# Transposing cached keys on VectorE in 32x32 blocks and scoring them as 32x32 products, in the decode attention of a hybrid decoder step

## The chip, the cores and the metric

One core of one Trainium2 chip runs the whole program; all data are f32. The metric is the device time of one execution in microseconds (us), the median of the runs. The core has TensorE (matrix products, out of weights that are loaded first; its results land in PSUM, 8 banks of 512 columns), VectorE, ScalarE and GpSimd for everything else, and DMA queues that SyncE (SP) and GpSimd fill.

## The reference, cut to what matters

The program is one layer of a decoder: RMS norm, one input projection, eight attention heads with forget gates beside eight RWKV-7 heads, an output projection, a SwiGLU network and a last norm. It is done for one prompt of 16 + 512 tokens and for eight running sequences of 8 new tokens each. The change is in the attention of the running sequences over their cached past:

```python
PAST_LEN = 4096; PAGE_SIZE = 128; FOX_HEADS = 8; HEAD_DIM = 64; DEC_BATCH = 8; DEC_SEQ = 8
k_past = cache_k[l][page_table].reshape(DB, n_pages * PAGE_SIZE, FOX_HEADS, HEAD_DIM)
v_past = cache_v[l][page_table].reshape(DB, n_pages * PAGE_SIZE, FOX_HEADS, HEAD_DIM)
s = jnp.einsum('bqhd,bkhd->bhqk', qf, k.astype(jnp.float32))
s = s + cq - jnp.swapaxes(c_k, 1, 2)[..., None, :]
p = jax.nn.softmax(jnp.concatenate(logits, axis=-1), axis=-1)
o = jnp.einsum('bhqk,bkhd->bqhd', p[..., start:start + n], v.astype(jnp.float32))
```

So for each of 8 sequences, 32 pages of 128 tokens (each 128 x 512 values of keys and as many of values) are read by number, and every page is scored against 8 heads x 8 queries.

## The kernel before

The program is written engine by engine, with semaphores, in these stages: the input projection and the prompt's attention (up to about 331 us), then the **lots stage** (335 to 912 us), then the output projection, the SwiGLU network (L1369, L1388, L1394) and the last norm.

**Lots.** The running sequences are taken in 4 pairs (`NPAIR`), each pair's 32 pages in 8 lots of 4 pages (`LOT`, `NLOT`), so 32 lots (`LOTS`). A page of a pair is a 128x512 tile for each of the two sequences (q). The 128 rows of scores are 2 sequences x 8 heads x 8 queries. In a lot TensorE does this:

- `turn_keys` (L1173) transposes each page with 4 products 128x128 by the identity into PSUM bank 0 or 1 (32 in a lot, L1178), and ScalarE copies them to SBUF in `take_keys` (L1617, L1622).
- `page_scores` (L1181) multiplies. Its weights are `QB`, 128 x 32: the two heads of group g over 128 rows. Its moving operand is 128 columns of the transposed keys; the output is one of four 32-row strips of bank `SCORE`. So it is a 128x32 tile of the array, four of them side by side, 8 in a page (L1192).
- `turn_probs` (L1214, L1218) transposes the probabilities of the lot before, and `lot_values` (L1230, L1237) multiplies them with the values. After it L1241 is one more product, of one column, over all four strips; it adds nothing the result needs and raises the semaphore `ov_ready` that VectorE waits for in `add_output`.

VectorE adds the forget terms (`add_scores`: L2100 add, L2103 maximum, L2107 sign), copies the turned probabilities (L2131) and adds up the output (L2141). ScalarE does the exponentials (`exp_lot`, L1628). SP loads the pages in `load_lot` (L441): each key page waits until `turn_keys` of the same slot in the lot before is done (`k_free`), each value page until `lot_values` is (`v_free`). The key ring holds one lot, as does the value ring.

**What sets the order.** Every engine runs a generator `all_lots` of 8 pieces a lot and between them the pieces of a second generator, `rwkv_rest` (the RWKV-7 heads of the prompt and of the running sequences, L1002, L992 and others). Both are interleaved by the same rule on all engines, so that each engine's queue holds a fixed order:

```python
def rwkv_due(piece):
    return min(N_RWKV, 1 + piece * (N_RWKV - 1) // (8 * LOTS - 20))
```

`N_RWKV` is 140, so there are 139 / 236 = 0.59 recurrent pieces behind each piece of a lot, until 2.5 lots before the end. An engine that waits in a piece holds up everything behind it.

## Time and profile before

| | us |
|---|---|
| median of 3 runs | 1509.98 (1507.31 to 1511.25) |
| the profiled execution, its time | 1510.73 |
| its span in the profile | 1509.0 |
| TensorE busy in the span | 1402.4 |
| VectorE / ScalarE / GpSimd busy | 438.2 / 357.0 / 110.0 |
| mean granted TensorE clock, share of full speed | 0.969 |

A window of the span is read by its busy times, a group of instructions by its count, its busy time and the mean time of one. Products overlap: the mean time of one is from its start to its end, and several tiles of the array run at once, so the busy time of a group is much less than count times mean. An x-count in the profile is of instructions as the chip ran them: an f32 product is two of them, a transpose by identity one.

### The profile page before, as it was taken

To read this page: it belongs to the slowest core of one execution; us is meant where nothing else is said; L and a number is where in the kernel's file an instruction comes from. 1 tells how busy PE (TensorE), PEld (TensorE's weight loads), DVE (VectorE), ACT (ScalarE), POOL (GpSimd) and SP (SyncE) were. 2 spreads that over 40 slices of the span, in tenths; PEclk is the share of its full clock that TensorE was granted. 3 is DMA by queue.
4 is the path that set the end of the run, shared out by engine and by line. 5 is a ranking of instruction groups with operands and counts; after the bars stand their busy time and mean duration, and the time that the engine had idled before them with its cause. 6 is when DMAs were issued, how large, how long until landed. Compare 5 with 4: busy or idle time off the path is not lost.

```text
span 1509.0 us, 27895 instructions
## 1 busy us (share of the span) xinstructions
PE 1402.4 (93%) x11595; PEld 953.3 (63%) x11595; DVE 438.2 (29%) x917; ACT 357.0 (24%) x713; POOL 110.0 (7%) x223
## 2 busy tenths in 40 slices
PE   5999999988799999999989779999999999999997
PEld 4755666655577777777755454477777777744442
DVE  5022355455844444444445241310000000000002
ACT  3010233245444343443433331100000000000011
POOL 6283000000000000001202010000000000000000
PEclk9999899998799999999989889999999999999998
DMA  5187011023898787878957897003111221150001
GB/s 206 57 189 205 7 57 35 1 75 110 284 312 277 229 292 247 294 255 266 272 191 261 315 314 245 1 13 100 56 56 56 89 79 56 56 195 0 0 0 63
DMA packets 123174, 219.32 MB, mean 145 GB/s; under 512 B 11451, under 2 KB 35078, under 8 KB 123046
## 3 DMA queue, kind: packets, MB, share of 16 engines
q1 hardware_dynamic: 115154, 193.64, 38.3%
q0 software_dynamic: 7824, 23.85, 5.9%
q8 instruction: 92, 1.51, 0.4%
q14 instruction: 36, 0.29, 0.1%
q10 hardware_dynamic: 68, 0.02, 0.0%
HBM read 203.06 MB, written 14.41 MB: 144 GB/s over the span
## 4 chain that ended last, share of the span: by engine, by line
PE 84%; DVE 5%; DMA 4%; ACT 3%; issue 2%; SPq 1%; POOL 0%; DVEq 0%; POOLq 0%; ACTq 0%
PE PS L1369 23%; PE PS L736 13%; PE PS L1388 10%; PE PS L1178 6%; PE PS L1192 4%; PE PS L1308 4%; PE PS L1237 4%; PE PS L709 2%; DMA arena<-in_cache_k 2%; DMA out_wkv_prompt<-arena 1%; PE PS L1394 1%; PE PS L992 1%; PE PS L1002 1%; PE PS L996 1%; ACT arena L1622 1%
## 5 line engine op out<-in xcount | busy, mean ns | idle before, releaser
L1369 PE MATMUL PS<-arena 128*128 128x288 f32 x1408 | 342.1, 405 | 1.2 <-DVE arena L2251 1.2
L1369 PEld LDWEIGHTS PS<-arena 128*128 128x128 f32 x1408 | 265.7, 189 | 77.4 <-DVE arena L2251 1.4
L736 PE MATMUL PS<-arena 128*128 128x301 f32 (+1 forms) x736 | 197.7, 426 | 0.0
L1622 ACT ACTIVATE arena<-PS 128x512 f32<-128x512 f32 x256 | 141.4, 596 | 192.8 <-PE PS L1178 192.4
L1178 PE MATMUL PS<-arena 128*128 128x128 f32 x1024 | 153.8, 296 | 27.1 <-DMA arena<-in_cache_k 15.1
L736 PEld LDWEIGHTS PS<-arena 128*128 128x128 f32 (+1 forms) x736 | 136.6, 189 | 54.7 <-issue 13.6
L1178 PEld LDWEIGHTS PS<-arena 128*128 128x128 f32 x1024 | 122.1, 151 | 55.8 <-issue 24.2
L1388 PE MATMUL PS<-arena 128*128 128x512 f32 x352 | 151.5, 592 | 1.5 <-DVE arena L2277 1.5
L1388 PEld LDWEIGHTS PS<-arena 128*128 128x128 f32 x352 | 66.5, 189 | 86.2 <-issue 84.3
L2277 DVE TENSOR_TENSOR arena<-PS,arena 128x576 f32<-128x576 f32 x22 | 16.7, 758 | 327.0 <-ACT arena L1686 327.0
L1686 ACT ACTIVATE arena<-PS 128x576 f32<-128x576 f32 x22 | 14.3, 651 | 329.8 <-PE PS L1369 329.8
L1192 PE MATMUL PS<-arena 128*32 128x128 f32 x2048 | 85.7, 286 | 3.8 <-ACT arena L1622 2.4
L1237 PE MATMUL PS<-arena 128*32 128x256 f32 x1024 | 69.7, 389 | 2.8 <-DMA arena<-in_cache_v 2.8
L1192 PEld LDWEIGHTS PS<-arena 128*32 128x32 f32 x2048 | 50.0, 112 | 24.8 <-issue 19.3
L1308 PE MATMUL PS<-arena 128*128 128x512 f32 x128 | 55.8, 593 | 0.0
L1952 DVE TENSOR_TENSOR arena<-PS,arena 128x512 f32<-128x512 f32 (+2 forms) x56 | 35.9, 659 | 41.3 <-PE PS L992 20.6
L2297 DVE TENSOR_TENSOR arena<-PS,arena 128x512 f32<-128x512 f32 x8 | 5.5, 692 | 143.2 <-PE PS L1388 143.2
L363 POOL DMA_DIRECT2D out_y_prompt<-arena x4 | 2.1, 537 | 596.0 <-DVE arena L2286 596.0
L1671 ACT ACTIVATE arena<-arena 128x1024 f32<-128x1024 f32 x8 | 8.4, 1045 | 151.4 <-DVE arena L2297 137.7
L1237 PEld LDWEIGHTS PS<-arena 128*32 128x32 f32 x1024 | 29.5, 111 | 22.3 <-issue 6.4
L1308 PEld LDWEIGHTS PS<-arena 128*128 128x128 f32 x128 | 23.9, 189 | 29.1 <-issue 29.1
L1434 ACT ACTIVATE arena<-PS 128x602 f32<-128x602 f32 (+1 forms) x23 | 15.5, 673 | 108.3 <-PE PS L736 108.3
(360 smaller groups left out, 1409.9 us busy)
## 6 DMA issues: line engine op xcount, KB each, us to landing
arena<-in_cache_k SPq DMA_DIRECT2D x256, 256.0 KB, 4.3
arena<-in_cache_v SPq DMA_DIRECT2D x256, 256.0 KB, 4.8
arena<-in_w_gate SPq DMA_DIRECT2D x11, 1024.0 KB
arena<-in_w_up SPq DMA_DIRECT2D x11, 1024.0 KB
arena<-in_w_in SPq DMA_DIRECT2D x5, 2048.0 KB, 11.9
forgets_after<-arena POOLq DMA_DIRECT2D x64, 128.0 KB, 8.5
arena<-forgets_after SPq DMA_DIRECT2D x32, 256.0 KB, 5.1
arena<-in_w_down SPq DMA_DIRECT2D x4, 2048.0 KB
```

Source lines behind the costliest of these rows:

```text
L709: ins = mm(o, xnT[:, k, 17 + P * (i - 1):17 + P * i], w, start=(k == 0), stop=(k == KT - 1))
L736: ins = mm(PS[0:width, bank, 0:HALF], wring[:, c % 2, k, c0:c0 + width], xnT[:, k, half * HALF:(half + 1) * HALF], start=(k == 0), stop=(k ...
L1178: ins = tr(PS[:, bank, g * P:(g + 1) * P], Kr[:, i, q, g * P:(g + 1) * P], ident)
L1192: ins = mm(PS[ROWS[2 * q + gp], SCORE, i * P:(i + 1) * P], QB[:, 2 * (L // NLOT) + q, g, :], KTs[:, (2 * i + q) % LOT, g, :], start=(gg == ...
L1237: ins = mm(PS[ROWS[r], OUT, 0:QW], PTs[:, i, ROWS[r]], Vr[:, i, r // 2, QW * (r % 2):QW * (r % 2) + QW], start=(i == 0), stop=(i == LOT - ...
L1308: ins = mm(PS[rows, E + 2 * (n % 2) + half, :], mixT[:, k, cols], wo[:, k, half * NB:(half + 1) * NB], start=(k == 0), stop=(k == KT - 1))
L1369: ins = mm(PS[:, 4 * (f % 2) + 2 * w + half, 0:HO], fring[r % FR][:, c:c + P], hT[:, k, half * HO:(half + 1) * HO], start=(k == 0), stop=( ...
L1388: ins = mm(PS[:, 4 * half + n, :], actT[:, k, cols], w_down(half, k), start=(k == 0), stop=(k == NF - 1))
L1434: av(dst.rearrange("p (a b) -> p a b", a=2), src, ACT.Copy, scale=scale).then_inc(S["proj_taken"], 1)
L1622: av(KTs[:, (2 * i + q) % LOT], PS[:, T_USE[("k", L, i, q)] % 2, :].rearrange("p (g n) -> p g n", g=NG), ACT.Copy)\
L1952: return tt(dst, src, mask.unsqueeze(1).unsqueeze(1).to_broadcast([n_p, a, b, n]), ALU.mult)
L2277: tt(actT[:, f, :].rearrange("p (a b) -> p a b", a=2), PS[:, 4 * (f % 2) + 2:4 * (f % 2) + 4, 0:HO], sgate[:, f % 2, :].rearrange("p (a b) ...
```

## The change

Keys are no longer transposed by TensorE. VectorE transposes them in place, in SBUF, in 32x32 blocks, and TensorE multiplies what results in 32x32 tiles:

- After a block transpose, partition 32a + d of a page holds dimension d of a half head for the 32 tokens of group a. A score is now a sum of two products with 32 rows, for each token group a and each head. Weights are `QS`, 32x32 with the 8 queries of one head in their own 8 columns and zeros elsewhere, so four heads (hm) and two half heads (d) are summed in one strip: 8 products behind each other on one output.
- `page_scores(L, hh, part)` takes half a lot (2 pages of both sequences), and in a part two of the four token groups: 64 products of 32x32 with 64 moving columns (2 pages x 32 tokens). The four parts of a lot are 256 products. The two token groups of a part write different PSUM banks (`SCORE` = [2, 1]); part 1 waits for the last product of part 0 (`sc_part`).
- `turn_keys(n, i)` on VectorE: 4 instructions of 128x1024 a lot, each after all four transfers of its half lot have landed.
- `take_keys` on ScalarE is gone; the copy of the turned probabilities goes from VectorE to ScalarE (`take_probs`). `add_scores` adds in two instructions, one for each bank.
- The key ring is three half lots (`KH`): a half lot is loaded once the half three before it has been scored. SP issues, in lot L: keys of the second half of L+1, the 8 values of L, the bias of L+1, keys of the first half of L+2.
- L1241 is gone; VectorE waits for `v_free` instead.
- ScalarE fills `QS` anew for each pair (`fill_queries`, 4 small copies), from `QX`, which VectorE lays out with 16 small copies in the prompt's attention (`spread_queries`) instead of 8 copies for `QB`. The scores of the new tokens are also 64 products of 32x32 for each pair. `exp_lot(L)` stands in lot L itself, at its seventh piece.
- The two small weights `w2`, `a2` are loaded to another place, after `log_ready`.

Cut to its core:

```diff
-            def turn_keys(L, i):
-                pe.wait_ge(k_in[i], 32 * (L + 1))
-                for q in range(2):
-                    bank = t_bank(("k", L, i, q))
-                    for g in range(NG):
-                        ins = tr(PS[:, bank, g * P:(g + 1) * P], Kr[:, i, q, g * P:(g + 1) * P], ident)
-                    ins.then_inc(S["k_free"], 1)
-
-            def page_scores(L, i):
...
-                pe.wait_ge(S["kt_taken"], 2 * LOT * L + 2 * i + 2)
-                for gg in range(2):
-                    for q in range(2):
-                        for gp in range(2):
-                            g = 2 * gp + gg
-                            ins = mm(PS[ROWS[2 * q + gp], SCORE, i * P:(i + 1) * P], QB[:, 2 * (L // NLOT) + q, g, :],
-                                     KTs[:, (2 * i + q) % LOT, g, :], start=(gg == 0), stop=(gg == 1), skip_group_check=True)
-                ins.then_inc(S["sc_page"], 1)
+            def page_scores(L, hh, part):
+                n = 2 * L + hh
+                if part == 0:
+                    if hh == 0:
+                        if L % NLOT == 0:
+                            pe.wait_ge(S["nmn_ready"], L // NLOT + 1)
+                        if L:
+                            pe.wait_ge(S["sc_taken"], 2 * L)
+                    pe.wait_ge(S["kt_ready"], 2 * n + 2)
+                else:
+                    pe.wait_ge(S["sc_part"], n + 1)
+                a0 = 2 * (part ^ hh)
+                for hm in range(4):
+                    for d in range(2):
+                        for a in (a0, a0 + 1):
+                            for q in range(2):
+                                for gp in range(2):
+                                    h = 4 * gp + hm
+                                    o = PS[ROWS[2 * q + gp], SCORE[a % 2], 2 * P * hh:2 * P * hh + 2 * P].rearrange("p (i n) -> p i n", i=2)
+                                    ins = mm(o[:, :, 32 * a:32 * a + 32], QS[ROWS[a], q, h, d],
+                                             KH[n % 3][ROWS[a], :, q, 64 * h + 32 * d:64 * h + 32 * d + 32],
+                                             start=(hm + d == 0), stop=(hm + d == 4), skip_group_check=True)
+                ins.then_inc(S["k_free"] if part else S["sc_part"], 1)
...
+            def turn_keys(n, i):
+                dve.wait_ge(k_in[n % 3], 64 * (n // 3 + 1))
+                pages = KH[n % 3][:, i].rearrange("p q n -> p (q n)")
+                v.transpose(pages, pages).then_inc(S["kt_ready"], 1)
...
-                tt(sv[:, 1:], PS[:, SCORE, :], Rr[:, j % 2, :], ALU.add).then_inc(S["sc_taken"], 1)
+                for a in range(2):
+                    tt(by_group(sv[:, 1:], a), by_group(PS[:, SCORE[a], :], a), by_group(Rr[:, j % 2, :], a), ALU.add).then_inc(S["sc_taken"], 1)
```

The pieces of a lot, on TensorE and on VectorE:

```diff
@@ TensorE, all_lots @@
-                    turn_keys(L, 0)
-                    yield
-                    turn_keys(L, 1)
-                    page_scores(L, 0)
-                    yield
+                    page_scores(L, 0, 0)
                     if L:
                         turn_probs(L - 1)
                     yield
-                    turn_keys(L, 2)
-                    page_scores(L, 1)
+                    page_scores(L, 0, 1)
                     yield
                     if L:
                         lot_values(L - 1, 0)
                     if j == 0:
                         turn_new(pr)
                     yield
-                    turn_keys(L, 3)
-                    page_scores(L, 2)
-                    yield
                     if L:
                         lot_values(L - 1, 1)
                     yield
-                    page_scores(L, 3)
+                    page_scores(L, 1, 0)
+                    yield
+                    if j == 0 and L:
+                        turn_output(pr - 1)
+                    page_scores(L, 1, 1)
+                    yield
@@ VectorE, all_lots @@
+                    turn_keys(2 * L + 1, 0)
+                    yield
+                    turn_keys(2 * L + 1, 1)
                     if L:
                         add_sums(L - 1)
                     yield
-                    if L:
-                        take_probs(L - 1)
-                    yield
                     yield
                     if j == 0:
                         take_new_probs(pr)
                     yield
-                    yield
                     if L:
                         add_output(L - 1)
...
+                    if L + 1 < LOTS:
+                        turn_keys(2 * L + 2, 0)
                     yield
                     add_scores(L)
+                    yield
+                    if L + 1 < LOTS:
+                        turn_keys(2 * L + 2, 1)
+                    yield
```

How the queues stand, from the built programs. A row is a line of code, the operation, output and input, the output's shape and how many stand behind each other. First TensorE, in the middle of the recurrence: one lot before (L1178 turns keys, L1192 scores, L1218 turns probabilities, L1237 values; L992, L996 and L1002 are the recurrence).

```order
L1178 MATMUL PS<-arena 128x128 x16
L1192 MATMUL PS<-arena 32x128 x8
L992 MATMUL PS<-arena 64x64 x8
L996 MATMUL PS<-arena 128x128 x4
L1218 MATMUL PS<-arena 128x128 x4
L1178 MATMUL PS<-arena 128x128 x8
L1192 MATMUL PS<-arena 32x128 x8
L1002 MATMUL PS<-arena 64x64 x8
L1237 MATMUL PS<-arena 32x256 x8
```

And with the change, in a like place: L1179 scores a part, L1210 turns probabilities, L1229 values, L979, L983 and L989 are the recurrence. The first row is the second part of a lot, the last but one the first part of the next.

```order
L1179 MATMUL PS<-arena 32x2x32 x64
L979 MATMUL PS<-arena 64x64 x8
L983 MATMUL PS<-arena 128x128 x4
L1229 MATMUL PS<-arena 32x256 x16
L989 MATMUL PS<-arena 64x64 x8
L1179 MATMUL PS<-arena 32x2x32 x64
L979 MATMUL PS<-arena 64x64 x8
L983 MATMUL PS<-arena 128x128 x4
L1179 MATMUL PS<-arena 32x2x32 x64
L989 MATMUL PS<-arena 64x64 x8
L1179 MATMUL PS<-arena 32x2x32 x64
L1210 MATMUL PS<-arena 128x128 x4
```

The groups of 8 and 16 transposes and their scores have become four blocks of 64 products; between the last part of a lot and the first of the next one recurrent piece stands here (L989).

On VectorE, around `add_scores` before (L2100, L2103, L2107; L1952 and L1981 take the recurrence's products, L2141 adds the output, L2125 and L2127 the sums):

```order
L1981 TENSOR_TENSOR arena<-PS,arena 128x2x4x64
L2141 SCALAR_TENSOR_TENSOR arena<-arena,PS 128x256
L1952 TENSOR_TENSOR arena<-PS,arena 128x512
L2100 TENSOR_TENSOR arena<-PS,arena 128x512
L2103 TENSOR_REDUCE arena<-arena 128x1
L2107 TENSOR_SCALAR arena<-arena 128x1
L1981 TENSOR_TENSOR arena<-PS,arena 128x2x4x64
```

and with the change (L2108, L2111, L2115 are `add_scores`, L1951 and L1980 the recurrence, L2147 the output):

```order
L2147 SCALAR_TENSOR_TENSOR arena<-arena,PS 128x256
L2097 STREAM_TRANSPOSE arena<-arena 128x1024
L1980 TENSOR_TENSOR arena<-PS,arena 128x2x4x64
L2108 TENSOR_TENSOR arena<-PS,arena 128x8x32 x2
L2111 TENSOR_REDUCE arena<-arena 128x1
L2115 TENSOR_SCALAR arena<-arena 128x1
L2097 STREAM_TRANSPOSE arena<-arena 128x1024
L1951 TENSOR_TENSOR arena<-PS,arena 128x512
```

A transpose now stands on each side of `add_scores`; the second one (the second two pages of the next lot's first half) comes behind it and ahead of the recurrence's next instruction.

## Rows read from the trace of the kernel before

**Rows 1.** The page: busy time of each engine, its share of the span, instructions.

```profile
PE 1402.4 (93%) x11595; PEld 953.3 (63%) x11595; DVE 438.2 (29%) x917; ACT 357.0 (24%) x713; POOL 110.0 (7%) x223
```

**Rows 2.** Windows of the span; columns as in the first line.

```profile
core 0: us, PE busy (x) PEld busy (x) DVE busy (x) ACT busy (x) POOL busy (x), PEclk, DMA share, GB/s
335.00:430.00 95.00, 79.39 (x760) 54.07 (x762) 61.37 (x73) 47.60 (x69) 1.75 (x5) 0.83 0.64 218
430.00:745.00 315.00, 299.39 (x5854) 234.91 (x5850) 135.48 (x286) 131.60 (x259) 13.36 (x17) 1.00 0.82 271
745.00:912.00 167.00, 136.42 (x1525) 89.61 (x1521) 65.46 (x125) 60.93 (x109) 11.43 (x18) 0.90 0.78 268
...
886.00:902.00 16.00, 9.16 (x113) 6.36 (x112) 2.71 (x5) 4.33 (x9) 0.51 (x1) 0.84 1.04 369
```

**Rows 3.** Groups of TensorE's products: busy us, mean ns, idle before.

```profile
L1178 PE MATMUL PS<-arena 128*128 128x128 f32 x1024 | 153.8, 296 | 27.1 <-DMA arena<-in_cache_k 15.1 <-DVE arena L2131 6.0 <-ACT arena L1622 4.2
L1192 PE MATMUL PS<-arena 128*32 128x128 f32 x2048 | 85.7, 286 | 3.8 <-ACT arena L1622 2.4 <-DVE arena L2118 1.4
...
L1241 PE MATMUL PS<-arena 128*128 128x1 f32 x64 | 12.3, 261 | 0.0
```

**Rows 4.** Waits of TensorE, 335 to 912 us: total, times, longest.

```profile
PE PS L1178 <- DMA arena<-in_cache_k: 15.1, 5, 5.3
PE PS L1178 <- DVE arena L2131: 6.0, 13, 1.2
```

**Rows 5.** The chain of waits at the start of the lots.

```profile
331.29 4.28 DMA arena<-in_cache_k
335.61 3.84 PE PS L1178 x16
```

**Rows 6.** The same windows for L1178, then L1237, then L1218 alone.

```profile
335.00:430.00 95.00, 27.27 (x152) 21.99 (x152) 0.83 0.64 218
430.00:745.00 315.00, 83.43 (x608) 65.99 (x608) 1.00 0.82 271
745.00:912.00 167.00, 43.13 (x264) 34.17 (x264) 0.90 0.78 268
...
430.00:745.00 315.00, 39.28 (x592) 16.56 (x592) 1.00 0.82 271
...
430.00:745.00 315.00, 11.98 (x76) 8.25 (x76) 1.00 0.82 271
```

**Rows 7.** Timeline, TensorE: start us, us, engine, line, shape, count.

```profile
625.29 0.65 PE L1192 MATMUL PS<-arena 128*32 128x128 f32 x16
...
625.87 0.69 PE L1002 MATMUL PS<-arena 64*64 64x64 f32 x32
...
634.47 0.15 PEld L1226 LDWEIGHTS PS<-arena 64*32 64x32 f32 x8 [0.17 <-issue]
...
635.04 1.14 PE L1024 MATMUL PS<-arena 64*64 64x64 f32 x16
```

**Rows 8.** L1002 and L1226 by themselves: ns min/median/max, first and last start.

```profile
L1002 PE MATMUL PS<-arena x736: 216/218/268, 429.6 to 741.8; 64*64 64x64 f32 x184
...
L1226 PEld LDWEIGHTS PS<-arena x32: 102/104/107, 352.8 to 779.0; 64*32 64x32 f32 x32
```

**Rows 9.** Groups of VectorE's instructions that price the new ones.

```profile
L2131 DVE COPY arena<-PS 128x512 f32<-128x512 f32 x32 | 22.1, 689 | 33.4 <-PE PS L1218 32.9 <-DVE arena L1981 0.3
L2103 DVE TENSOR_REDUCE arena<-arena 128x1 f32<-128x513 f32 x32 | 22.0, 687 | 1.1
...
L1888 DVE TENSOR_TENSOR_SCAN arena<-arena 128x640 f32<-128x640 f32 x4 | 5.6, 1472 | 0.3 <-ACT arena L1495 0.3
...
L2107 DVE TENSOR_SCALAR arena<-arena 128x1 f32<-128x1 f32 x32 | 4.9, 154 | 1.1
...
L1952 DVE TENSOR_TENSOR arena<-PS,arena 128x256 f32<-128x256 f32 x6 | 2.5, 423 | 3.1 <-PE PS L992 3.1
...
L2091 DVE TENSOR_TENSOR arena<-arena 128x2048 f32<-128x2048 f32 x1 | 2.3, 2294 | 0.0
```

250 lines of the change are left out of this document (123 added, 127 removed).

## The prediction

> **What bounds the kernel now.** I read the page first: TensorE is busy 1402 of 1509 us [rows 1]. The change touches only the lots stage, so the windows come next [rows 2]. It falls into three stretches. From 430 to 745 us, where the recurrence runs beside the lots, TensorE is busy 299 of 315 us at the full clock (granted share 1.00, 2.4 GHz) and VectorE 135: TensorE bounds it. From 335 to 430 us TensorE is busy 79 of 95 us and VectorE 61; each waits for the other in turn. From 745 to 912 us TensorE is busy 136 of 167. The counts of L1178 (32 transposes a lot) say how many lots fall in each: 152, 608 and 264 of 1024, so 4.75, 19 and 8.25 lots [rows 6]. In the middle a lot takes 315/19 = 16.6 us. DMA moves 271 GB/s there, 85.4 MB or 4.5 MB a lot, and the busiest window shows 369 GB/s [rows 2]. So DMA has room, but not much: at 12.2 us a lot it would be full. TensorE's waits are short: 15.1 us for keys in all, 6.0 us for VectorE's copy of the probabilities [rows 4].
>
> **TensorE: what goes.** Transposes 153.8 us, scores 85.7, the one-column products 12.3 [rows 3]: 251.8 us, or 7.9 us a lot.
>
> **TensorE: what comes.** A part is 64 f32 products, 128 instructions as the chip runs them, and there are 128 parts. Their price is the open question, for no row shows 32x32 tiles. Three rows bound it. L1024 sends 16 products of 64 columns through the same tile: (1.14 - 0.22)/15 = 61 ns from one to the next. L1002 sends 32 of the same length through four tiles in turn: (0.69 - 0.22)/31 = 15.2 ns, a quarter [rows 7, 8]. A part keeps eight tiles in turn. If eight overlap as four do, the price is 61/8 = 7.6 ns. The issue of instructions must keep up with that: L1226 loads 8 weights in 0.15 us when one takes 0.104, so they start (0.15 - 0.104)/7 = 6.6 ns apart, with a product between two loads [rows 7, 8]. That is just enough. I take 7.6 ns, since both rows allow it; the ends are 6.6 and 15.2. A part is then 127 x 0.0076 + 0.22 = 1.19 us and the four of a lot 4.8, with the new tokens' scores (four blocks of 64 in all) 4.9 us. The saving is 3.0 us a lot.
>
> A rule of the Trainium skill speaks against this. "TensorE: Matmul & The Clock Gate", section "Wait — 56ns, not 53.3ns?", says that matmuls start no less than about 25 ns apart, however short they are. The trace disagrees at four tiles, with 15.2 ns [rows 7].
>
> **VectorE and ScalarE.** VectorE gets 128 transposes of 128x1024. A two-operand instruction of 2048 columns takes 2.29 us, so 1.15 us for 1024; the slowest row that works along the columns, the scan, takes 1.47 us for 640, so 2.36 us for 1024 [rows 9]. I take 1.15, as a transpose reads one operand and keeps no running value, and keep 2.36 as the upper end; the lower is 1.15 less the 0.15 that one column costs, 1.0 us. A lot thus adds 4.6 us and loses the copy of 0.69 [rows 9]. In the middle VectorE rises from 135 to about 135 + 19 x 3.9 + 19 x 0.15 = 212 us, which fits. ScalarE loses its copies of keys and takes over one; it waits for TensorE now and I cost it at nothing. The 16 small copies of the query layout lie in the prompt's stage, beside products, and cost nothing there; should that cover be gone, they cost 16 times between 0.15 and 0.42 us [rows 9].
>
> **The wait that takes the place.** Before, the transposes of a lot's first pages needed nothing but their data, so TensorE always had work at a lot's border. Now the first part of a lot needs `turn_keys(2L+2, 1)`, which VectorE issues behind `add_scores(L)`, which waits for the last part of the lot before. The chain is 2 x 0.42 (halves of 128x256) + 0.69 (maximum) + 0.15 (sign) + 1.15 (transpose) [rows 9] and some 0.15 for five handovers: 3.0 us. Behind TensorE's last part stand only recurrent pieces, 3 x 0.59 = 1.8 of them on the mean. One costs (299.4 - 19 x 7.9 - 39.3 - 12.0)/(19 x 8 x 0.59) = 1.1 us [rows 2, 6], so the cover is 1.9 us, and 1.1 us a lot is given back. The recurrence's own step on VectorE also comes behind a transpose, as the order shows; I put 0.3 us a lot on that. The wait for part 0 (`sc_part`) is in the 0.22 us of a part.
>
> **Keys' transfers.** A half lot is freed in the second or sixth piece of a lot and needed in the first or fifth of the next: 7 pieces, over 12 us, against some 4.3 us for a transfer to land [rows 5]. SP issues as many transfers as before, in another order. While `turn_keys` waits for keys, the recurrence's next step on VectorE waits behind it, and TensorE for that; before, TensorE alone waited. I cost the ring at nothing; its cover goes if a lot comes near 12.2 us. At the start, VectorE needs all four transfers of a half lot and two transposes before TensorE scores: 3 us more than the 4.28 us that the chain shows now [rows 5].
>
> **The sum.** Middle: 19 x (-3.0 + 1.1 + 0.3) = -30, of which I take -28, since DMA must then move 85.4 MB in 287 us, 298 GB/s. Last stretch: -3.0 + 1.5 (fewer recurrent pieces cover, none in the last 2.5 lots) over 8.25 lots is -12; part of it waits for transfers and for the recurrence's states anyway: -10. First stretch: VectorE stands in the chain and gets 4.75 x 3.9 = 18 us in 95; TensorE's 14 us saved lie mostly in its idle time: +6. Start: +3. In all -29: 1510.7 - 29 = 1482 us for the execution profiled, whose time is 0.7 us over the median, so **1482 us**. By the 25 ns of the Trainium skill's page on the clock gate a part would be 3.4 us and the sum 32 x (4 x 3.4 + 0.2 - 7.9 + 1.4) = +234 us, an estimate.
>
> **Rivals.** *Products don't overlap eight deep* (slower). If eight tiles give no more than four, 15.2 ns, a part is 2.15 us, a lot 8.8, so +0.9 and with the new waits +2.3 us a lot: 1511 + 74 + 3 = 1588. It decides from (3.0 - 1.4)/512 instructions = 3.1 ns over my price, 10.7 ns, and near 10 ns with the first stretch. For it: f32 products come in twos on one tile, and the two token groups double what must be held back at once. Against: four tiles reach the full quarter. The same would follow if small tiles brought the granted clock down, which four-tile blocks don't: 1.00 in the middle. Chance 0.20. *VectorE becomes the bound*: transposes at 2.36 us. The middle would hold 212 + 76 x 1.21 = 304 us of VectorE, so some 325; first stretch +20, last +5 on my terms' place: about 1546. Chance 0.12. The Trainium skill's "VectorE: DVE Perf Modes", section "The three transpose paths", gives 311 ns for 128 columns of bf16, which would be 2.5 us here; its "Vector Engine (DVE) Microarchitecture Reference", section 3.8, says one element per cycle and lane. No row shows which. *The waits are covered*: the recurrence fills the border of the lots, and the saving of 3.0 us a lot stands until DMA stops it. Middle -45, last -20, start and first 0: 1446. Chance 0.20. *A product costs its start, not its columns*: L1192's 128 columns in four tiles start (0.65 - 0.29)/15 = 24 ns apart [rows 3, 7]; were that a floor for 32x32 tiles too, a part would be 3.3 us and the stage 32 x (13.2 + 0.1 - 7.9 + 1.4) = 218 us longer, some 1735 in all. L1002's 15.2 ns are against it. Chance 0.02. The floor of the Trainium skill's "TensorE: Matmul & The Clock Gate" would be this rival. *The change gives back exactly what it takes*: 1511, chance 0.04. That it doesn't do what it says is excluded by the order of the queues: L1178's transposes are gone.
>
> **How the numbers follow.** The forecast has 0.42 and its own range 1460 to 1505. A measurement of this kernel can tell 0.3%, 4.5 us, from no change. Faster: 0.40 of the forecast's 0.42 and the 0.20 of the covered waits, 0.60; within: 0.06; slower: 0.34. The range, 1438 to 1555, takes in the covered case, VectorE as the bound and half of the first rival, and leaves out its dearest half and the case of the floor.
>
> **What the profile would show.** A block of 64 scores at 1.2 us (2.15 for the rival); a transpose at 1.15 us; TensorE's longest waits in the lots stage for VectorE's transpose, once a lot, about 1.1 us; the stage 335 to 912 shortened to some 548 us, most of it in the middle; a granted clock still 1.00 there; all after it (L1369, L1388) unchanged. I am wrong if the blocks take 1.6 us or more, if VectorE is over 85% busy in the middle, or if keys come late.

## The result, and the profile after

| | us |
|---|---|
| median after, 4 runs | 1809.41 (1798.29 to 1815.63) |
| median before, 4 runs beside them | 1510.62 (1507.31 to 1512.75) |
| ratio, with 95% interval | 1.197 (1.191 to 1.204) |
| span of the profiled execution | 1796.6 |
| TensorE / VectorE / ScalarE busy | 1540.4 / 569.5 / 243.9 |
| mean granted TensorE clock | 0.832 |

The change makes the kernel 299 us slower; the prediction said 28 us faster and is outside its range on the other side. The windows of the changed kernel's span show where the time went (busy us and counts of PE, PEld, DVE, ACT, POOL, then granted clock, DMA share, GB/s):

```profile
335.00:430.00 95.00, 66.13 (x1974) 43.14 (x1974) 70.21 (x77) 25.93 (x29) 0.00 (x0) 0.66 0.50 167
430.00:745.00 315.00, 245.02 (x8455) 193.81 (x8454) 133.48 (x228) 40.71 (x83) 1.75 (x5) 0.68 0.52 172
745.00:1200.00 455.00, 343.00 (x11285) 248.41 (x11286) 188.68 (x322) 60.24 (x115) 24.77 (x35) 0.67 0.57 187
335.00:1200.00 865.00, 654.16 (x21713) 485.36 (x21714) 392.38 (x626) 126.87 (x227) 26.52 (x40) 0.67 0.55 180
1200.00:1796.00 596.00, 582.32 (x2084) 370.27 (x2082) 48.33 (x86) 32.45 (x65) 3.26 (x6) 0.99 0.18 59
```

The profiled execution, the shortest of the four, is 288 us longer than before's. All of it lies in the lots stage, 577 us before [rows 2] and 865 now, 27.0 us a lot in place of 18.0. The rest is as it was: 596 us at clock 0.99 behind the stage, against 597 before. In the stage nothing looks full. TensorE is busy 76%, VectorE 45%, DMA moves less than before [rows 2]. But the granted clock is 0.67, between the two levels, where it had been 1.00 in the middle, and TensorE works on 43426 instructions (products and weight loads) instead of 16248: 1357 a lot instead of 508.

The groups and the waits of the changed kernel (L1179 are the score products, L1229 the values, L1210 the turned probabilities, L2097 VectorE's transposes). First the groups:

```profile
L1179 PE MATMUL PS<-arena 32*32 32x64 f32 x16384 | 249.4, 267 | 165.2 <-issue 134.6 <-DVE arena L2097 23.2 <-DVE arena L2128 5.6
L1229 PE MATMUL PS<-arena 128*32 128x256 f32 x992 | 92.5, 515 | 2.7 <-issue 2.6
L1210 PE MATMUL PS<-arena 128*128 128x128 f32 x124 | 30.9, 396 | 0.0
...
L2097 DVE STREAM_TRANSPOSE arena<-arena 128x1024 f32<-128x1024 f32 x128 | 155.8, 1232 | 8.5 <-DMA arena<-in_cache_k 7.9
```

Then TensorE's waits in the stage (us in total, times, longest us):

```profile
PE PS L1179 <- issue: 134.6, 67, 5.3
PE PS L1179 <- DVE arena L2097: 23.2, 10, 5.7
PE PS L979 <- issue: 7.4, 4, 3.4
```

The scores take 249.4 us, as much as transposes, scores and one-column products took before, 251.8 [rows 3]. The new wait is one that I had not named: "issue", time in which the engine waited for nothing that the profile shows. On the page it is 10% of the chain that ended last, where it was 2%. The transposes on VectorE, which I had thought the danger, are waited for 23 us in all.

The timeline of TensorE shows what such a wait looks like (start us, us, line, shape, count, idle before):

```profile
599.92 2.41 PE L1179 MATMUL PS<-arena 32*32 32x64 f32 x128 [4.00 <-issue]
603.41 0.47 PE L1179 MATMUL PS<-arena 32*32 32x64 f32 x17 [1.07 <-issue]
...
610.37 2.04 PE L1179 MATMUL PS<-arena 32*32 32x64 f32 x128
...
622.35 1.48 PE L1179 MATMUL PS<-arena 32*32 32x64 f32 x128
623.76 0.69 PE L967 MATMUL PS<-arena 64*64 64x64 f32 x32
624.38 0.43 PE L1179 MATMUL PS<-arena 32*32 32x64 f32 x25
627.98 1.34 PE L1179 MATMUL PS<-arena 32*32 32x64 f32 x103 [3.17 <-issue]
629.25 1.00 PE L979 MATMUL PS<-arena 64*64 64x64 f32 x25
631.82 0.49 PE L979 MATMUL PS<-arena 64*64 64x64 f32 x7 [1.57 <-issue]
```

A part of 128 products (and their 128 loads) takes 1.48 us at the full clock and 2.04 at the lower one, if it is whole. Many are cut in the middle, without a wait in the program there: 25, then nothing for 3.17 us, then 103. And the pieces between two stops have a fixed length: 103 + 25 = 128 products and as many weight loads, **256 TensorE instructions**; the stretch from 599.92 to the stop at 602.3 has 128 and 128 again. The stop is not at a certain place of the program; it falls in L979, a product of the recurrence, just as well. The queue that the page calls instruction shows the other side. Before:

```profile
q8 instruction: 92, 1.51, 0.4%
```

After:

```profile
q8 instruction: 198, 3.24, 0.7%
```

3.24 MB in 198 packets are 16 KB a packet, and the 27392 further TensorE instructions (13696 products and as many loads) came with 106 packets: 258 instructions each. So TensorE's program itself comes by DMA, 256 instructions at a time. In the raw trace of the stage the packets of this queue start 3.3 us apart at best, with a median of 4.5 us, and each takes about 1 us. After a long stop TensorE mostly starts again 2.3 to 2.6 us behind the start of a packet. Of the 55 distances between stops of over 1.9 us, 34 are a whole multiple of 128 products, to within 4; the others are mixed with waits for semaphores. Before, no two packets started less than 4.2 us apart in the stage (median 7.1), and TensorE waited for issue once, 0.6 us. At 3.7 us, a packet in a busy spell, 256 instructions come at 14 ns each, and TensorE, at the full clock, works a part off at 1.48/256 = 5.8 ns each. The Trainium skill's "Runtime: NRT & Kernel Launch", section "Instruction fetch mechanics", says that each sequencer fetches its code by its own DMA queue in 16 KiB blocks of 256 instructions, and that the cost is "mostly hidden". The trace agrees with the blocks and disagrees with hidden: 134.6 us at one line.

So there were two suspects in the stage's 288 us. TensorE's busy time other than scores rose from 515 - 252 = 263 us to 654 - 249 - 5 (new tokens) - 3 (products of the output projection that the window takes in) = 397, by 134 us, for the same products: L1237 took 389 ns each, L1229 now 515. That is the clock: in the raw trace, such a product that starts at the full clock takes 383 ns on the mean in either kernel, and one that starts at the lower clock some 624; before, 32 of 1024 started at the lower clock, now 541. Its idle time rose from 577 - 515 = 62 to 865 - 654 = 211 us, by 149; that is mostly the arrival of instructions, since the waits for issue on all lines make 158 us, and made 0.6 before. The two make 283 of 288. This is bookkeeping, not yet proof: the order of the queues and VectorE's new part had changed as well.

### The profile page after: what moved, and what is told of

Same layout as the page of the kernel before. It is cut to its first block, busy times and chain, and to the rows that moved or that the text cites. A ratio compares the mean times of both kernels' runs of the same rounds, so it can differ in the third digit from the quotient of the medians.

```text
span 1796.6 us, 54490 instructions
## 1 busy us (share of the span) xinstructions
PE 1540.4 (86%) x25291; PEld 1059.6 (59%) x25291; DVE 569.5 (32%) x1059; ACT 243.9 (14%) x505; POOL 109.8 (6%) x222
## 3 DMA queue, kind: packets, MB, share of 16 engines
q8 instruction: 198, 3.24, 0.7%
## 4 chain that ended last, share of the span: by engine, by line
PE 83%; issue 10%; DVE 5%; ACT 1%; DMA 0%; SPq 0%; POOL 0%; DVEq 0%; POOLq 0%
PE PS L1355 19%; PE PS L1179 13%; PE PS L723 10%; PE PS L1374 8%; PE PS L1229 5%; PE PS L1294 3%; PE PS L1210 2%; PE PS L696 2%; PE PS L979 1%; PE PS L983 1%; PE PS L989 1%; PE PS L1380 1%; DVE arena L2097 1%; PE PS L937 1%; PE PS L1031 1%
## 5 line engine op out<-in xcount | busy, mean ns | idle before, releaser
L1179 PE MATMUL PS<-arena 32*32 32x64 f32 x16384 | 249.4, 267 | 165.2 <-issue 134.6
L1179 PEld LDWEIGHTS PS<-arena 32*32 32x32 f32 x16384 | 209.0, 124 | 216.0 <-issue 201.5
L1355 PEld LDWEIGHTS PS<-arena 128*128 128x128 f32 x1408 | 265.7, 189 | 77.4 <-DVE arena L2262 1.4
L2097 DVE STREAM_TRANSPOSE arena<-arena 128x1024 f32<-128x1024 f32 x128 | 155.8, 1232 | 8.5 <-DMA arena<-in_cache_k 7.9
L1374 PEld LDWEIGHTS PS<-arena 128*128 128x128 f32 x352 | 66.4, 189 | 86.3 <-issue 84.3
L1229 PE MATMUL PS<-arena 128*32 128x256 f32 x1024 | 94.4, 511 | 2.7 <-issue 2.6
L2108 DVE TENSOR_TENSOR arena<-PS,arena 128x256 f32<-128x256 f32 x64 | 24.3, 420 | 144.9 <-PE PS L1179 140.6
L1951 DVE TENSOR_TENSOR arena<-PS,arena 128x512 f32<-128x512 f32 (+2 forms) x56 | 35.8, 656 | 82.5 <-PE PS L979 53.0
L1229 PEld LDWEIGHTS PS<-arena 128*32 128x32 f32 x1024 | 35.7, 138 | 43.8 <-issue 36.8
L1621 ACT ACTIVATE arena<-arena 128x513 f32<-128x513 f32 x32 | 23.1, 721 | 188.6 <-DVE arena L2115 188.6
L1294 PEld LDWEIGHTS PS<-arena 128*128 128x128 f32 x128 | 24.8, 197 | 30.9 <-issue 30.9
L583 POOL DMA_DIRECT2D forgets_after<-arena x64 | 37.0, 589 | 45.4 <-DVE arena L1762 31.0
L1980 DVE TENSOR_TENSOR arena<-PS,arena 128x512 f32<-128x512 f32 (+1 forms) x26 | 17.9, 688 | 64.3 <-PE PS L989 64.1
```

The source lines that it names most:

```text
L583: pool.dma_start(forgets_after[b, DS * h:DS * h + DS].rearrange("t (c k) -> c t k", k=PAGE), src)\
L1179: ins = mm(o[:, :, 32 * a:32 * a + 32], QS[ROWS[a], q, h, d], KH[n % 3][ROWS[a], :, q, 64 * h + 32 * d:64 * h + 32 * d + 32], start=(hm + ...
L1229: ins = mm(PS[ROWS[r], OUT, 0:QW], PTs[:, i, ROWS[r]], Vr[:, i, r // 2, QW * (r % 2):QW * (r % 2) + QW], start=(i == 0), stop=(i == LOT - ...
L1294: ins = mm(PS[rows, E + 2 * (n % 2) + half, :], mixT[:, k, cols], wo[:, k, half * NB:(half + 1) * NB], start=(k == 0), stop=(k == KT - 1))
L1355: ins = mm(PS[:, 4 * (f % 2) + 2 * w + half, 0:HO], fring[r % FR][:, c:c + P], hT[:, k, half * HO:(half + 1) * HO], start=(k == 0), stop=( ...
L1374: ins = mm(PS[:, 4 * half + n, :], actT[:, k, cols], w_down(half, k), start=(k == 0), stop=(k == NF - 1))
```

## Experiments

**Fewer instructions for the same columns.** `e1_wide` puts the two half heads of a score in one product of 128 columns, so half of the products are gone; half of the contraction's weights are left out.

```diff
-                    for d in range(2):
+                    for d in range(1):
...
-                                    ins = mm(o[:, :, 32 * a:32 * a + 32], QS[ROWS[a], q, h, d],
-                                             KH[n % 3][ROWS[a], :, q, 64 * h + 32 * d:64 * h + 32 * d + 32],
+                                    ins = mm(o[:, :, 64 * (a // 2):64 * (a // 2) + 64], QS[ROWS[a], q, h, d],
+                                             KH[n % 3][ROWS[a], :, q, 64 * h:64 * h + 64],
```

> The changed kernel, but the two half heads of a head go as one product of 128 columns with the weights of the first half: 128 products of 32x32 tiles a lot instead of 256, with the same number of streamed columns; the second half head's weights are left out, so the scores are not the reference's. Theory F (TensorE's instructions arrive too slowly: its gaps in the changed kernel stand at every 256th instruction, and its packets of 16 KB of instructions come at best some 3.7 us apart): a lot falls from 1357 to about 845 instructions, 3.3 packets or 12 us, which is less than a lot; the gaps inside blocks go, the granted clock returns to about 1.00 in the middle, and the time falls to 1480 to 1540 us. Theory T (small tiles themselves are what costs, by their price and by a clock that they bring down): the columns streamed through 32x32 tiles are the same, so the clock stays near 0.67 in the stage and the time stays above 1650 us. Theory V (VectorE's transpose at the border of the lots): nothing changes there, above 1700 us.

Measured: 1644.7 us, ratio to before 1.088 (1.083 to 1.093): 165 us less than the changed kernel at the same streamed columns. It lies between what I had expected of the two theories, under 1540 and over 1650. Much less of it is waiting for instructions:

```profile
PE PS L1179 <- issue: 22.8, 16, 2.6
```

On all lines the waits for issue in the stage fell from 158 to 50 us. But the granted clock is 0.70 there and not near 1.00, and TensorE's products other than the scores are busy 398 us, as in the changed kernel (405, and 263 before). So most of the 134 us that this run is slower than before is not the arrival of instructions.

**The same instructions for half the columns.** `e2_narrow` keeps all 256 products of a lot and gives each 32 columns instead of 64 (one page instead of two; the other scores are left out).

> The changed kernel with each product cut from 64 to 32 columns (the first half head for one page, the second for the other), so half the multiplications are left out and the number of instructions is the same. Theory F: the gaps stay where they are, at every 256th instruction, and the time stays within 40 us of the changed kernel, 1770 to 1830. Theory T: with half the columns a block of 64 products takes less, and if columns set its price the time falls by 128 x 0.6 to 0.7 = 80 us or more, to 1730 or less, unless the clock falls further. Theory V: within 20 us of the changed kernel.

Measured: 1802.3 us, ratio 1.192 (1.187 to 1.197), which is the changed kernel's time. A whole part at the full clock took 1.29 us instead of 1.48, and the stage is as long as the changed kernel's. Its wait in the groups:

```profile
L1179 PE MATMUL PS<-arena 32*32 32x32 f32 x16384 | 200.8, 224 | 189.0 <-issue 159.1 <-DVE arena L2097 22.7 <-DVE arena L2128 5.2
```

The scores' busy time fell by 49 us and their wait for instructions rose by 25. Over the whole stage TensorE is busy 35 us less and waits 35 us longer for issue (193 us). With this many instructions the stage is paced by their number and not by what they stream.

**Less traffic of the pages.** `e3_light` transfers 64 of the 512 columns of each key and value page (the rest is stale).

```diff
-                        sp.dma_start(KH[n % 3][:, i, q, :], k_pages[...]...)
+                        sp.dma_start(KH[n % 3][:, i, q, 0:64], k_pages[..., :, 0:64]...)
```

> The changed kernel with key and value transfers of the first 64 of 512 columns (descriptors of 256 bytes instead of 2 KB; an eighth of the bytes; the rest of each page is stale, so the attention is not the reference's). If instruction packets are slow because they share the DMA engines with the pages (theory F with contention): packets come 2 us apart or less, gaps shrink to under 1 us and the time falls under 1600 us. If a packet has a time of its own, whatever else moves (theory F, fixed): gaps stay, 1750 to 1810 us. Theory V: keys never come late, but the time stays above 1750.

Measured: 1741.6 us (one run), 68 less, between what I had expected of contention and of a fixed time. The waits for issue at L1179 fell from 134.6 us (67 times, longest 5.3) to 77.5 (58 times, longest 3.3), but the packets of instructions still start 3.3 us apart at best. So the page traffic makes some packets late; their own shortest period stays without it.

**Small instructions in the kernel before.** This is the run that decides. `e7_small_in_before` is the kernel before, unchanged in order, waits and VectorE's work, in which each group of four key transposes is replaced by 30 products of 32x32 over four tiles (the scores read garbage).

```diff
-                    for g in range(NG):
-                        ins = tr(PS[:, bank, g * P:(g + 1) * P], Kr[:, i, q, g * P:(g + 1) * P], ident)
+                    for m in range(30):
+                        a, r, c = m % 4, m % 4, slice(32 * (m % 16), 32 * (m % 16) + 32)
+                        ins = mm(PS[ROWS[r], bank, c], ident[ROWS[a], 0:32], Kr[ROWS[a], i, q, c], start=True, stop=True, skip_group_check=True)
```

> The kernel before, in which each group of 4 key transposes (128x128) is replaced by 30 products of 32x32 with 32 columns on the diagonal tiles; so the scores read keys that are not transposed. A lot then has about 1340 TensorE instructions in place of 508 and, at 7.6 to 15 ns an instruction, 3.6 to 7.3 us of small products in place of 4.8 us of transposes. No VectorE transpose, no new wait, the order of before. Theory (arrival of instructions): gaps at every 256th instruction, a granted clock in the stage well under 1.00, 1620 to 1790 us. Rival (the new waits for VectorE and the order of the changed kernel cause the loss): 1490 to 1530 us, or at most 1590 if the diagonal products take 15 ns, at clock 1.00.

Measured: 1780.1 us, ratio 1.177 (1.169 to 1.185). (I had miscounted there: a transpose is one product and one load, so the lot has 508 - 64 + 960 = 1404 instructions, not 1340.) The groups and two stretches of its timeline:

```profile
L1179 PE MATMUL PS<-arena 32*32 32x32 f32 x15360 | 201.3, 208 | 122.8 <-issue 111.3
```

```profile
522.26 0.96 PE L1179 MATMUL PS<-arena 32*32 32x32 f32 x87
527.03 2.11 PE L1179 MATMUL PS<-arena 32*32 32x32 f32 x127 [3.82 <-issue]
531.13 0.58 PE L1179 MATMUL PS<-arena 32*32 32x32 f32 x26 [1.99 <-issue]
```

The 15360 small products are busy 47 us more than the 1024 transposes they replace (153.8 [rows 3]), and the kernel is 266 us slower than the kernel before that was measured beside it. The stops are the same, a packet of 256 apart (127 products and their loads between two). Neither the 32x32 scores nor VectorE's transposes nor the new order of the queues is needed for the loss: many small TensorE instructions are enough.

The stage of this run, 850 us, divides as the changed kernel's did. TensorE's idle time is 199 us in place of 62, with 169 us of waits for issue on all lines. The small products cost 47 us more than the transposes, and all other products 449 us in place of 361, at a granted clock of 0.81. So the arrival of instructions is about half of this loss, too.

**The dose.** `e8_few_in_before` and `e12_mid_in_before` are the same with 12 and 21 products in place of the 30.

> As the run with 30 small products in the place of each group of 4 key transposes, but with 12: some 764 TensorE instructions a lot, and about 2.8 us a lot less work for TensorE than before. Theory (a packet of 256 instructions takes 3.7 us or more to come, and in practice the stage ran at 1.37 times that): 764/256 x 3.7 x 1.37 = 15.1 us a lot, so near before's pace: 1480 to 1540 us. Rival (count of instructions is nothing until a lot has over 1000 of them): TensorE's saved 2.8 us a lot come through, 1420 to 1460 us.

> The same with 21 small products for each group: some 1052 TensorE instructions a lot, 1.2 us a lot less work than before. Theory: 1052/256 x 3.7 x 1.37 = 20.8 us a lot against some 18 now, so 1590 to 1680 us, about half way to the 1780 of 30 products. Rival (a threshold near 1300): 1470 to 1530 us.

Measured: 1579.6 us, ratio 1.046 (1.032 to 1.059), and 1662.3, ratio 1.100 (1.095 to 1.106). The counts must be corrected in the same way, to 828 and 1116 a lot. The middle run is as expected. The small one is above both theories: there is no threshold near 1000. 828/256 packets of 3.7 us are 12 us, well under the lot's 18, and still L1179 waited 24.1 us for issue in 19 pieces, at a clock of 0.83. A mean rate that fits is not enough. The likely reason, which no run isolates, is that a burst of small instructions uses up the little that has been fetched ahead.

**VectorE taken out.** `e9_no_turn` is the changed kernel without VectorE's transposes; TensorE waits for the transfers instead and scores untransposed keys.

```diff
-                    pe.wait_ge(S["kt_ready"], 2 * n + 2)
+                    pe.wait_ge(k_in[n % 3], 64 * (n // 3 + 1))
...
-                dve.wait_ge(k_in[n % 3], 64 * (n // 3 + 1))
-                pages = KH[n % 3][:, i].rearrange("p q n -> p (q n)")
-                v.transpose(pages, pages).then_inc(S["kt_ready"], 1)
+                pass
```

> The changed kernel without VectorE's transposes: TensorE waits for the keys' transfers instead, and scores untransposed keys. VectorE loses 156 us and the wait at the lot's border. Theory (arrival of instructions): TensorE's instruction count is the same, so 1750 to 1800 us, the gaps stay. Rival (VectorE's chain): a fall by more than 100 us, to under 1700.

Measured: 1806.4 us, ratio 1.194 (1.184 to 1.205): 156 us of VectorE's work and its waits are gone, and the time is 3 us under the changed kernel's, which the noise covers. While TensorE is short of instructions, VectorE costs nothing that can be measured.

**Down to before's count.** `e5_quarter` and `e6_eighth` are `e1_wide` with two and one of the four head steps, so 589 and 461 instructions a lot.

```diff
-                for hm in range(4):
+                for hm in range(1):
```

> The merged products of the wide run, of which two of the four head steps are left out: 64 products a lot in place of 512 half-sized ones' 256, so the lot has some 590 TensorE instructions (changed kernel 1357, wide run 845, before 508). VectorE's transposes and all waits stay. Theory (arrival of instructions): the gaps at every 256th instruction go, the granted clock in the stage returns towards 1.00, and as TensorE then has less work than before, 1430 to 1500 us. Rival (VectorE's transposes and the wait at the lot's border hold the wide run at 1645): they are unchanged, so over 1580 us. Second rival (only the number of products counts, each at a fixed price, straight line through 1809 and 1645): 1645 - 164 x 64/128 = 1563 us.

> As the quarter run, with one of the four head steps: 32 products a lot, some 461 TensorE instructions, fewer than before's 508. VectorE's transposes and all waits stay. Theory (arrival of instructions): nothing is left to win against the quarter run but the products' own time, 1420 to 1490 us, clock 1.00 in the stage. Rival (VectorE's transposes and the border's wait): over 1580 us still. Straight line: 1522 us.

Measured: 1529.4 and 1509.7 us (one run each). Neither the theory nor its rival had this; the straight line through the counts (1563 and 1522) was nearest. The time falls by 115 and 135 us below `e1_wide`, so VectorE is not what held that run. These two don't show the price of an instruction, though: the work goes with the count. The scores' busy time falls from 199 us to 108 and 69, by 91 and 130 us, and the waits for issue on all lines only from 50 to 20 and 11. And at 461 instructions and some 6 us a lot less of TensorE work than before, it should have gone below before's time, and didn't. What holds it is in its waits, the longest first:

```profile
PE PS L1179 <- DVE arena L2097: 39.3, 16, 9.6
PE PS L1229 <- DMA arena<-in_cache_v: 8.3, 5, 4.1
PE PS L1229 <- ACT arena L1605: 7.8, 6, 4.4
```

and in its clock. Of the first row 14.7 us are two waits before 430 us, 8.4 us are seven waits in the middle, and 16.2 us seven waits after it. VectorE in its turn waited 18.8 us for keys (5 times, longest 6.6). The clock is 0.82 in the middle:

```profile
430.00:745.00 315.00, 257.40 (x5500) 180.80 (x5496) 215.44 (x380) 66.59 (x138) 15.03 (x22) 0.82 0.80 271
```

`e11_eighth_no_turn` and `e10_wide_no_turn` take VectorE's transposes out of `e6_eighth` and `e1_wide`.

> The run with 32 products a lot (1510 us) without VectorE's transposes. It prices my step of the prediction on the wait at the lot's border where instructions are not short. If the step holds (1.1 to 1.5 us a lot, and VectorE's share of the first stretch): 1440 to 1480 us. If VectorE and its waits cost nothing: 1500 to 1515 us. If most of what keeps this run at before's time is VectorE: under 1430 us, with the granted clock back at 1.00 in the stage.

> The wide run (128 merged products a lot, 1645 us) without VectorE's transposes: scores of untransposed keys. If what remains there of the loss is the clock and the arrival of instructions: 1620 to 1650 us. If it is VectorE's transposes and the border's wait (L1179 waited 29 us for them), 1550 to 1610 us.

Measured: 1469.6 us, ratio 0.973 (0.968 to 0.978), so 40 us less than with the transposes (of which there is one run); and 1620.1, ratio 1.072 (1.067 to 1.077), 25 less. That is the price of VectorE's transposes and of all waits for them, where late instructions no longer hide it: 1.25 us a lot on the mean.

**The clock.** It stayed at 0.82 where hardly an instruction was late, so I asked whether it is a cost of its own. Four dense dummy products a lot (512 columns through the whole array, into the bank that the transposes of probabilities then overwrite) were added to `e6_eighth` and to the changed kernel.

```diff
                 bank = t_bank(("p", L))
+                for i in range(4):
+                    mm(PS[:, bank, :], ident, Sb[:, L % 2, 1:1 + 4 * P], start=True, stop=True, skip_group_check=True)
```

> The run with 32 products a lot (1510 us, clock 0.83 in the stage), with four dense dummy products (128x128 by 512 columns, 8 TensorE instructions) added in each lot ahead of the transposes of the probabilities. At the full clock they take 8 x 0.43 = 3.4 us a lot, 107 us in all (31 lots). Theory (the low clock is a cost of its own, and comes from little streaming work): the clock in the stage returns to 0.9 or more, the rest of the work gets faster, and the time rises by less than 50 us: 1510 to 1560. Rival (the clock doesn't depend on it or costs nothing): 1600 to 1640 us.

> The changed kernel with the same four dense dummy products a lot (107 us of work at the full clock, 160 at the changed kernel's 0.67; only 16 instructions a lot more). Theory (clock and arrival are two costs): the clock rises above 0.8, part of the dummy work is paid back by the faster rest and part hides the instructions' arrival, since instructions come while the dense products run: 1780 to 1850 us. Rival (only arrival counts, the clock is free): the dense work also fills the gaps, so it would be nearly free too, 1800 to 1820, but with the clock unchanged. Third (both costs are independent of it): the work is added in full, 1910 to 1970 us.

Measured: 1591.4 us, ratio 1.053 (1.047 to 1.058), and 1898.2, ratio 1.256 (1.250 to 1.261), so 82 and 89 us more. Both lie between the theories. In `e13_eighth_filled` the granted clock of the middle is 0.88 in place of 0.82, and of the whole stage 0.83 in place of 0.75, not the 0.9 that I had expected:

```profile
430.00:745.00 315.00, 266.34 (x4820) 167.07 (x4816) 180.63 (x320) 55.96 (x117) 1.75 (x5) 0.88 0.68 232
```

The groups of `e13_eighth_filled` (L1210 is the dummy, L1231 the values):

```profile
L1210 PE MATMUL PS<-arena 128*128 128x512 f32 x256 | 164.4, 802 | 0.6 <-DVE arena L2169 0.6
L1231 PE MATMUL PS<-arena 128*32 128x256 f32 x1024 | 66.7, 387 | 5.7 <-ACT arena L1607 5.2 <-DMA arena<-in_cache_v 0.5
```

And the same values in `e6_eighth`:

```profile
L1229 PE MATMUL PS<-arena 128*32 128x256 f32 x1024 | 88.2, 483 | 16.2 <-DMA arena<-in_cache_v 8.3 <-ACT arena L1605 7.8
```

What runs behind the dense work has the full clock again: 387 ns, as 389 before. But the dummies have a price, 164 us in place of the 107 that I had set for the full clock, since they start at the low one: the first of the eight of a lot takes 1046 ns on the mean, the last 592. The rest of TensorE's work in the stage takes some 73 us less, 364 in place of 437. So the low clock has a price of its own, and dense work brings the clock back, at more than it returns. In `e14_after_filled` the stage has 0.75 instead of 0.67 and the waits for issue don't shrink (169 us on all lines, 158 without the dummies): the instructions behind the dense products are late all the same.

**One part of the change alone.** `e4_no_one_column` is the kernel before without the one-column product; VectorE waits for `v_free`. Nothing of the result is left out.

```diff
-                if half:
-                    mm(PS[:, OUT, 511:512], ident, ones[:, 0:1], start=False, stop=True, skip_group_check=True).then_inc(S["ov_ready"], 1)
...
-                dve.wait_ge(S["ov_ready"], L + L // NLOT + 2)
+                dve.wait_ge(S["v_free"], LOT * (L + 2))
```

> The kernel before with one part of the change alone: the one-column product behind each lot's values is gone and VectorE waits for v_free instead. It cost 12.3 us of TensorE's busy time, and TensorE bounds the middle. Theory of the prediction's sum: 7 to 12 us faster, 1499 to 1504. Rival (it fills time that TensorE would wait anyway, or only its latency is in the 12.3 us): within 0.3%.

Measured: 1507.1 us, ratio 0.9956 (0.9934 to 0.9978) over 12 runs against 17: 6.6 us faster by the ratio, 4.6 between the medians, just under the 7 to 12 expected. The interval lies under 1, but reaches into the rival's 0.3%. It is the fastest kernel here that leaves nothing of the result out.

The runs by the TensorE instructions of a lot:

| run | instructions a lot | VectorE transposes | us |
|---|---|---|---|
| `e11_eighth_no_turn` | 461 | no | 1469.6 |
| `e6_eighth` | 461 | yes | 1509.7 |
| before | 508 | no | 1510.6 |
| `e5_quarter` | 589 | yes | 1529.4 |
| `e8_few_in_before` | 828 | no | 1579.6 |
| `e10_wide_no_turn` | 845 | no | 1620.1 |
| `e1_wide` | 845 | yes | 1644.7 |
| `e12_mid_in_before` | 1116 | no | 1662.3 |
| `e9_no_turn` | 1357 | no | 1806.4 |
| changed kernel | 1357 | yes | 1809.4 |
| `e7_small_in_before` | 1404 | no | 1780.1 |

The table orders the runs by their count; the score work differs too, so it is no curve of the arrival alone. The three runs made from the kernel before with small products differ in nothing but their number. From 828 to 1116 an instruction costs 82.7 us / (288 x 32) = 9.0 ns, from 1116 to 1404 it costs 12.8 ns. That is all of its cost, its own work included: in the first step TensorE's busy time in the stage rises by 69 us and its idle time by 23, in the second by 52 and 68.

## Why the prediction was wrong, step by step

**The step that failed: "the issue of instructions must keep up with that".** I asked only how fast TensorE starts instructions that it has. The row of L1226, eight loads 6.6 ns apart [rows 7, 8], is a short burst, and it was right as such; I took it as a rate that could be held for 1357 instructions a lot. The sum has a term for the products' durations and none for the arrival of the instructions, that is, it puts that at nothing. I had counted 512 score products a lot and left out their 512 loads. The page before had the count to see, 92 packets, to which the change adds 106. The period was not there to see, since no two packets started less than 4.2 us apart and TensorE did not wait for them. At the 3.7 us of the changed kernel they take 1357/256 x 3.7 = 19.6 us a lot, against 287/19 = 15.1 in the middle of my forecast and 548/32 = 17.1 in its stage. Even that is too little: the stage took 27.0. Of the rest the pages' traffic accounts for 68 us or 2.1 us a lot (`e3_light`, one run); that the clock and the unevenness of the queue make the remainder is argued and not measured apart.

**"A granted clock still 1.00 there".** It was 0.67. I had named it beside the first rival ("small tiles brought the granted clock down") and dismissed it with the four-tile blocks. Wrong. Few small tiles go with a low clock too: `e6_eighth`, with an eighth of the score instructions, has 0.82 in the middle. In the kernel before TensorE was busy 95% of the middle, 83 us of it with 128x128 transposes of keys [rows 2, 6]. In every run without those transposes the clock is lower, and 128x256 products take 515 ns instead of 389 in the changed kernel. Late instructions, idle time and the missing dense work come together in these runs; `e13_eighth_filled` shows that dense work raises the clock, and no run shows how much of the fall is due to each of the three. The bookkeeping puts the price at 134 us.

**The price of a product, 7.6 ns.** (1.48 - 0.22)/127 = 9.9 ns in an undisturbed part. The eight tiles do overlap more than four (15.2), not fully. The first rival was to decide from 10.7, or near 10 with the first stretch, so this term alone, +0.3 us in each of 128 parts or 37 us, would have made it about no change; `e2_narrow` shows that even 8.4 ns ((1.29 - 0.22)/127) would not have helped. At the lower clock a part takes 2.04 us, over the 1.6 that I had named as a sign of being wrong. The rivals of a dear start, 24 and 25 ns, are refuted; the Trainium skill's rule in "TensorE: Matmul & The Clock Gate", section "Wait — 56ns, not 53.3ns?", that matmuls start no less than about 25 ns apart, does not hold across eight tiles. The time that I worked out from it, +234 us, came nearest to the measured +299, but by luck: no part that ran without a stop inside took the 3.4 us of that estimate; they took 1.47 to 2.47, most of them 1.48 or 2.04.

**VectorE's transposes, 1.15 us.** 1.23 us. Right; VectorE as the bound is refuted (`e9_no_turn`: -3 us for all of its new work). That is 1.20 ns a column, beside 1.12 of the two-operand row that gave the price (2.29/2048 [rows 9]). The Trainium skill's "Vector Engine (DVE) Microarchitecture Reference", section 3.8, says one element per cycle and lane; no run measures VectorE's cycle, but a steady pace near that of other instructions agrees with it. The 2.5 us that I had estimated from the 311 ns in the Trainium skill's "VectorE: DVE Perf Modes", section "The three transpose paths", is twice the measured time.

**The wait at the lot's border, 1.1 + 0.3 us a lot.** The mechanism exists, and the sum came near: 40 us, or 1.25 us a lot, in the pair `e6_eighth` and `e11_eighth_no_turn`; 25 us in the wide pair; 3 us, within the noise, in the changed kernel. But it is not the steady 1.1 us at every border that I had drawn. In the middle `e6_eighth` waits so in 7 pieces, 8.4 us in all, in place of 19 x 1.1 = 21, and the changed kernel in 2 pieces, 2.9 us; the longest wait, 9.6 us, lies in the first stretch. That the sum fits is in part luck. The three numbers do say that a wait is worth its full price only where nothing else is short.

**The key ring costs nothing.** TensorE never waited for keys itself in the changed kernel, and L2097 only 7.9 us. At 180 GB/s that was hardly a test. In `e6_eighth`, at 267 GB/s, VectorE waited 18.8 us for keys, so at the pace that I had forecast the term would not have been nothing.

**"TensorE: what goes", 7.9 us a lot.** The busy time is gone as I counted, and it would not have come back as time even with the instructions on time: `e6_eighth` spends 2.1 us a lot on scores instead of 7.9, and stands at before's time. In its stage TensorE's busy time fell only from 515 to 437 us, since all the rest ran slower (263 to 362), and its idle time rose from 62 to 139. I had let TensorE's saving come through one to one because it was the bound; the clock takes back part of what is saved, and the chains over VectorE and ScalarE another.

What stays open is the split. The clock's 134 us and the idle 149 us are read from one trace, and the two may hang together: a stop for instructions is also idle time. `e6_eighth` and `e13_eighth_filled` show that the low clock costs something with hardly a late instruction. No run has late instructions and a full clock; the nearest is `e7_small_in_before`, with 169 us of waits for issue at 0.81.

## What to carry to other kernels

Count the instructions of a change, not only their durations, and set the count against the instruction queue's packets in the profile: here 256 instructions took 3.3 us or more to come, so a stage that needs them faster than one in 13 to 14 ns stands, and bursts stood already at a mean of one in 24 ns (638 us for 32 x 828). A change from few large products to many small tiles must keep the count; half as many products of twice the columns was worth 165 us, 108 of them waits for issue, and halving their columns nothing. And work taken from a TensorE that holds the full clock is not returned in full: look at what the granted clock does when the dense part of the work is gone.

## What the runs showed of the hardware beyond that

- TensorE's stops for instructions lie whole blocks of 256 instructions apart, wherever that is in the program, and last up to 5.3 us in the changed kernel. Not every block ends in one: 82 waits for issue in 170 packets.
- A product 128x256 of f32 takes 383 ns at the full clock and some 624 at the lower one, in the kernel before as in the changed one.
- Products of 32x32 over eight tiles start 9.9 ns apart at the full clock with 64 columns, 8.4 with 32, and 13.6 at the lower ((2.04 - 0.31)/127).
- VectorE's block transpose takes 1.23 us for 128x1024 f32 whatever runs beside it (1194 to 1248 ns over the 128 of the changed kernel, 1193 to 1248 in `e6_eighth`).
- The same VectorE transposes and the waits for them are worth 3, 25 and 40 us in kernels that differ only in TensorE's score products.
